# Moving the subtraction between the MLP's two products from VectorE to GpSimd

## What is computed

```
hid = jnp.square(jax.nn.relu(hn @ w_up))     # 1024 -> 4096
x   = x + hid @ w_down                        # 4096 -> 1024
```

## Time and profile before

| what | value |
|---|---|
| median of three executions | 1307.18 us (1299.17 to 1309.70) |
| profiled execution, span from first to last instruction | 1308.3 us |
| PE busy | 1250.8 us, 96% of the span |
| DVE busy | 679.0 us, 52% |
| POOL busy | 482.7 us, 37% |
| ACT busy | 430.3 us, 33% |

### The profile page before, as it was taken

One profiled execution on the slowest core, in us unless ns is written; L12 is line 12 of the kernel. 1 busy time (PEld: TensorE's weight loads), 2 busy tenths in 40 slices (PEclk: granted clock), 3 DMA queues, 4 the chain that ended last, 5 costly groups with the idle time before them and its releaser, 6 DMA issues.

```text
span 1308.3 us, 17577 instructions
## 1 busy us (share of the span) xinstructions
PE 1250.8 (96%) x6316; PEld 1036.0 (79%) x6316; DVE 679.0 (52%) x975; ACT 430.3 (33%) x764; POOL 482.7 (37%) x286
## 2 busy tenths in 40 slices
PE   5899999999898999999988999999999999999997
PEld 4787777688676888888878888888798888888886
DVE  5544366525997775875355711785672131321315
ACT  5444233235311423322334110442443232241331
POOL 3444111044233445344444323420235435344340
PEclk9999699999988999999988999999999999999999
DMA  6423000033553565565322311302223223323211
GB/s 210 130 81 111 3 2 1 1 99 128 161 163 111 199 212 169 182 219 177 113 97 92 111 65 65 90 1 81 65 101 125 82 92 103 110 74 118 80 51 64
DMA packets 71065, 135.32 MB, mean 103 GB/s; under 512 B 6947, under 2 KB 9763, under 8 KB 70987
## 3 DMA queue, kind: packets, MB, share of 16 engines
q1 hardware_dynamic: 53636, 98.10, 22.9%
q10 hardware_dynamic: 17358, 36.27, 8.4%
HBM read 131.44 MB, written 2.13 MB: 102 GB/s over the span
## 4 chain that ended last, share of the span: by engine, by line
PE 74%; DVE 13%; issue 6%; ACT 3%; POOL 2%; DMA 1%; ACTq 0%; DVEq 0%; POOLq 0%
PE gemm L874 21%; PE gemm L876 21%; PE gemm L875 21%; DVE mod_acc L1505 4%; POOL w_lo L442 2%; PE aux L1049 2%; PE aux L1233 2%; PE gemm L1012 1%; PE gemm L1004 1%; PE aux L1039 1%; PE aux L922 1%; PE gemm L1014 1%; DVE nmax L1620 1%; PE gemm L1193 1%; DVE prob_t L1387 1%
## 5 line engine op out<-in xcount | busy, mean ns | idle before, releaser
L442 POOL TENSOR_TENSOR w_lo<-w_raw,w_hi 128x1024 fp32r<-128x1024 f32 (+1 forms) x180 | 448.6, 2513 | 643.1 <-ACT w_hi L656 404.6
L874 PE MATMUL gemm<-xt_hi,w_hi 128*128 128x512 f32 (+1 forms) x704 | 256.8, 365 | 7.0 <-issue 4.9
L875 PE MATMUL gemm<-xt_lo,w_hi 128*128 128x512 f32 (+1 forms) x704 | 255.3, 363 | 0.0
L876 PE MATMUL gemm<-xt_hi,w_lo 128*128 128x512 f32 (+1 forms) x704 | 255.3, 363 | 0.0
L874 PE MATMUL gemm<-w_hi,ht_hi 128*128 128x512 f32 x512 | 203.2, 397 | 6.0 <-POOL w_lo L442 6.0
L875 PE MATMUL gemm<-w_lo,ht_hi 128*128 128x512 f32 x512 | 202.1, 395 | 0.0
L876 PE MATMUL gemm<-w_hi,ht_lo 128*128 128x512 f32 x512 | 202.0, 395 | 0.0
L656 ACT ACTIVATE w_hi<-w_raw 128x1024 fp32r<-128x1024 f32 x124 | 125.5, 1050 | 206.3 <-PE gemm L876 120.6
L874 PEld LDWEIGHTS gemm<-xt_hi,w_hi 128*128 128x128 f32 x704 | 134.7, 191 | 28.7 <-issue 6.1
L875 PEld LDWEIGHTS gemm<-xt_lo,w_hi 128*128 128x128 f32 x704 | 134.7, 191 | 20.1
L876 PEld LDWEIGHTS gemm<-xt_hi,w_lo 128*128 128x128 f32 x704 | 134.5, 191 | 20.2
(11 more groups left out here) (192 smaller groups left out, 1477.4 us busy)
## 6 DMA issues: line engine op xcount, KB each, us to landing
wm<-in_w_mod ACTq DMA_DIRECT2D x48, 512.0 KB, 4.5
w_raw<-in_w_in SPq DMA_DIRECT2D x32, 512.0 KB, 3.7
w_raw<-in_w_up SPq DMA_DIRECT2D x32, 512.0 KB, 3.6
w_raw<-in_w_down SPq DMA_DIRECT2D x32, 512.0 KB, 3.6
w_raw<-in_w_mlp_in SPq DMA_DIRECT2D x32, 512.0 KB, 3.7
w_raw<-in_w_mlp_out SPq DMA_DIRECT2D x32, 512.0 KB, 3.5
w_raw<-in_w_out SPq DMA_DIRECT2D x16, 512.0 KB, 3.5
x<-in_x SPq DMA_DIRECT2D x4, 512.0 KB, 7.7
```

Of the source, the lines that this page charges most:

```text
L442: pool.tensor_tensor(w_lo[s % 2][:, ks, 0:width], raw[q][:, :, 0:width], w_hi[s % 2][:, ks, 0:width].bitcast(F32), ALU.subtract).then_inc( ...
L874: pe.matmul(bank, lh, rh, start=(k == 0), stop=False)
L875: pe.matmul(bank, lh, rl, start=False, stop=False)
L876: mm = pe.matmul(bank, ll, rh, start=False, stop=(k == KT - 1))
```

## The change

The work between the two products is divided anew. ACT's second operation writes the unrounded square into `hid`. DVE makes `ht_hi` by one copy, which rounds. POOL makes `ht_lo` by the subtraction that DVE did. The relu's wait for `hid_hi` goes; the square waits until `ht_lo` of two tiles before is done, as `hid` has two buffers; ACT's wait at the end of the up tiles is for `hid_lo`. POOL's loop is written anew: `low(c)` of each chunk in the order before, with `hid_low(c - 1)`, the subtraction for tile c - 1, behind `low(c)` for c = 1 to 7, and `hid_low(7)` ahead of `low(8)`.

```diff
+            def hid_low(c, i, up0):
+                pool.wait_ge(hid_hi, i * 8 + (up0 + c + 1))
+                pool.tensor_tensor(ht_lo[:, c, :], hid[c % 2][:], ht_hi[:, c, :].bitcast(F32),
+                                   ALU.subtract).then_inc(hid_lo, 1)
+            def mlp(s0, up0, more):
+                def chunk(i, splits):
+                    for c in range(splits):
+                        s, q = s0 + c // 4 + 1, c % 4
+                        if c == 8:
+                            hid_low(7, i, up0)
+                        low(s, q, NC, i * 16 + (4 * s + q + 1))
+                        if 1 <= c < 8:
+                            hid_low(c - 1, i, up0)
+                with pool.Fori(0, NCH if more else NCH - 1) as i:
+                    chunk(i, 16)
+                if not more:
+                    chunk(NCH - 1, 12)
...
-            lows(SLAB_OUT1 + 1, SLAB_OUT2 - SLAB_OUT1)
+            lows(SLAB_OUT1 + 1, 2)
+            mlp(SLAB_MLP1, 0, True)
+            lows(SLAB_IN2 + 1, 4)
...
-            lows(SLAB_MLP2, SLABS - SLAB_MLP2)
+            lows(SLAB_MLP2, 1)
+            mlp(SLAB_MLP2, 8 * NCH, False)
...
                     if c >= 2:
                         act.wait_ge(hid_ready, i * 8 + (up0 + c - 1))
-                        act.wait_ge(hid_hi, i * 8 + (up0 + c - 1))
                     act.activation(relu[c % 2][:], gp[(t0 + c) % 4][:], ACT.Relu).then_inc(relu_done, 1)
                     act.wait_ge(relu_done, i * 8 + (up0 + c + 1))
-                    act.activation(ht_hi[:, c, :], relu[c % 2][:], ACT.Square).then_inc(hid_hi, 1)
+                    if c >= 2:
+                        act.wait_ge(hid_lo, i * 8 + (up0 + c - 1))
+                    act.activation(hid[c % 2][:], relu[c % 2][:], ACT.Square).then_inc(hid_ready, 1)
...
                     act.wait_ge(hid_ready, i * 8 + (up0 + 8))
-                    act.wait_ge(hid_hi, i * 8 + (up0 + 8))
+                    act.wait_ge(hid_lo, i * 8 + (up0 + 8))
...
-                            dve.wait_ge(relu_done, i * 8 + (up0 + c + 1))
-                            if c >= 2:
-                                dve.wait_ge(hid_lo, i * 8 + (up0 + c - 1))
-                            dve.tensor_tensor(hid[c % 2][:], relu[c % 2][:], relu[c % 2][:], ALU.mult
-                                              ).then_inc(hid_ready, 1)
-                            dve.wait_ge(hid_hi, i * 8 + (up0 + c + 1))
                             dve.wait_ge(hid_ready, i * 8 + (up0 + c + 1))
-                            dve.tensor_tensor(ht_lo[:, c, :], hid[c % 2][:], ht_hi[:, c, :].bitcast(F32),
-                                              ALU.subtract).then_inc(hid_lo, 1)
+                            dve.tensor_copy(ht_hi[:, c, :], hid[c % 2][:]).then_inc(hid_hi, 1)
```

More of the change, by code:

```diff
@@ L445, in lows @@
             def lows(first, slabs):
[L447 to L451, removed]
-                    for q in range(UQ):
-                        low(first + slabs - 1, q, NC, 4 * (first + slabs - 1) + q + 1)
+                for s in range(first, first + slabs):
+                    for q in range(UQ):
+                        low(s, q, NC, 4 * s + q + 1)
+            def hid_low(c, i, up0):
[15 more added lines that the diff above has]
+                    chunk(NCH - 1, 12)
             def clear_pads(q_pad, count):
@@ L1452, in chunk @@
                         if c < 8:
-                            dve.wait_ge(relu_done, i * 8 + (up0 + c + 1))
-                            if c >= 2:
-                                dve.wait_ge(hid_lo, i * 8 + (up0 + c - 1))
-                            dve.tensor_tensor(hid[c % 2][:], relu[c % 2][:], relu[c % 2][:], ALU.mult
-                                              ).then_inc(hid_ready, 1)
-                            dve.wait_ge(hid_hi, i * 8 + (up0 + c + 1))
                             dve.wait_ge(hid_ready, i * 8 + (up0 + c + 1))
-                            dve.tensor_tensor(ht_lo[:, c, :], hid[c % 2][:], ht_hi[:, c, :].bitcast(F32),
-                                              ALU.subtract).then_inc(hid_lo, 1)
+                            dve.tensor_copy(ht_hi[:, c, :], hid[c % 2][:]).then_inc(hid_hi, 1)
                         else:
                             dve.wait_ge(gemm_done, i * 16 + (t0 + c + 1))
-                            if c == 8:
-                                dve.wait_ge(hid_lo, i * 8 + (up0 + 8))
                             cols = acc[:, c % 4, (c // 4 - 2) * NC:(c // 4 - 1) * NC]
```

## The result

| | before | after |
|---|---|---|
| median of the runs | 1303.18 us (16 runs, 1296.41 to 1313.06) | 1315.53 us (16 runs, 1311.55 to 1326.60) |
| ratio | 1 | **1.0105** [1.0074, 1.0137] |
| DVE busy in the profiled execution | 679.0 us | 602.8 us |
| POOL busy | 482.7 us | 572.3 us |
| PE busy | 1250.8 us | 1240.7 us |

The change costs 12.35 us by the medians, where 12.6 us was forecast. One thing must be known to read the times: the executions of every kernel here fall into two groups 11 to 12 us apart. In the seven profiled executions whose time is of the lower group the first relu of the first MLP starts between 309.5 and 312.7 us, in the five of the upper group between 321.9 and 324.7, and those five have a stretch of 24 to 34 us at half clock from 140 us on. I call them **early** and **late**; the executions without a trace are sorted by their time alone.

The account below looks back on a forecast made before the run. PE was taken as the bound, except in the first MLP's chunk 0, where DVE's modulations set the pace. 6.8 + 2.8 + 1.7 + 1.3 = 12.6 us on 1307.2 gave 1319.8 us, range 1306 to 1327.

Parts of the forecast that it names:

- Tile 8 in seven chunks: PE's tile 8 waits 0.91 to 0.99 us for tile 6's subtraction behind low(7); together 6.8 us.
- Tile 4 in the second MLP: Chunk 0 there: two subtractions ahead of low(3) hold PE 2.8 us, and half clock after the pause costs 1.7 us.
- Chunk 0 of the first MLP: DVE's gain and loss cancel; tile 8 waits one more subtraction, +1.3 us, bounds -9.1 and +4.
- It is hidden by DVE's own lag: First MLP's chunk 0: tile 4 is held about 3 us, but DVE reaches it over 4 us behind relu.
- The two cancel to 0.7 us: First MLP's chunk 0: DVE saves 7.4 us and loses 8.1 us; DVE's short idle times cover the rest.
- The holding: First MLP's chunk 0: eight POOL subtractions each slow DVE's two-input accumulations by 1.0 us, 8.1 us in all.
- DVE's relief: First MLP's chunk 0: one copy replaces two DVE operations in each of eight tiles, saving 7.4 us.
- The skill's rule: First MLP's chunk 0: DVE fully blocked by each subtraction, 10.2 us lost, total 1321.9; the forecast used eight tenths instead.
- DVE's relief in chunk 0: Rival, first MLP: DVE keeps its 7.4 us, PE's waits shrink, a half-speed stretch goes; 1309.4 us, chance 0.20.
- The waits breed more: Rival: tile 4's delay shows in first-MLP chunks 0 and 1, or clock falls; 1325, dearest form 1332; chance 0.18.
- Never reaches PE: Rival: the new order does not delay PE, as when tile 7 ends later than read; 1307 us, chance 0.07.
- ACT's longer wait at the end of the up tiles: Some 1.7 us longer, hidden because tile 12 needs the splits behind it only 21.8 us later.

Follow-up runs that it names:

- e2: Changed kernel with ACT making splits 5, 6 and 7 one tile earlier, so low(7) ends before tile 6 needs POOL; ratio 1.0102 to the kernel before.
- e3: Changed kernel with both edits of order: subtractions for tiles 0 to 2 behind low(3), and splits 5 to 7 one tile earlier; ratio 0.9998 to the kernel before.
- e7: Changed kernel with POOL's subtraction for tile 6 ahead of low(7) instead of behind it; ratio 1.0071 to the kernel before.
- e6: Changed kernel with each of POOL's subtractions made twice in a row, the second one signalling; ratio 1.0376 to the kernel before.
- e1: Changed kernel with POOL's subtractions for tiles 0 to 2 moved behind low(3); ratio 1.0104 to the kernel before.
- e5: Changed kernel with each POOL subtraction covering 8 of 512 columns, the third pass reading ht_hi for ht_lo, order and waits kept; ratio 0.9952 to the kernel before.
- e10: e9 with ACT's splits 5 to 7 one tile earlier; ratio 0.9963 to the kernel before.
- e8: Kernel before the change with only ACT's splits 5 to 7 made one tile earlier; ratio 0.9968 to the kernel before.
- e4: Changed kernel with the subtraction back on DVE, DVE's copy kept and POOL left with its lows; ratio 0.9987 to the kernel before.
- e9: Changed kernel with ACT squaring twice, unrounded and rounded, DVE only subtracting and POOL left with its lows; ratio 0.9984 to the kernel before.

## Why the prediction was right, point by point

- **Tile 8 in seven chunks, 6.8 us: right.** The working gave 0.98 us in the second MLP; the chunks grew by 0.86, 0.86 and 0.95. In chunks 1 and 2 of the first MLP it was 1.21 and 1.25 instead of 0.91, since the subtraction there took 1.72 us (at 458.32) beside DVE's accumulations. e2 and e3 take it away in the second MLP, e7 takes a third off it there and e6 enlarges it.
- **Tile 4 in the second MLP, 4.5 us: right, 3.97 measured** (first relu to the eighth, 29.88 to 33.85 us). The wait was 2.36 us instead of 2.8. The first copy was held as forecast (1.05 us long, from 961.17) and its subtraction started 0.36 us after `low(1)`, 0.5 in the working; the second copy delayed `low(2)` by 0.2 us (2.59 long) instead of 0.5. The half clock was one stretch of 3.4 us, the 1.7 us taken. e1 removes all of it.
- **Chunk 0 of the first MLP, +1.3 us: the step that failed.** It was +3.95. "It is hidden by DVE's own lag" is wrong: tile 4 came out of a wait of 3.63 us (323.43), DVE began on that tile 23.7 us after the first relu (at 335.06) where it had been 20.9 (342.89), and the eight up tiles took 38.58 us instead of 35.87; the rest of the chunk, with tile 8, took 73.30 instead of 72.06. "The two cancel to 0.7 us" is wrong as well, by one of its two sizes. The holding was about right, 0.94 us each and 7.5 in all against 8.1. DVE's relief, forecast at 7.4 us, is worth 2.3 at most: nearly without the holding (e5) the chunk is only that much shorter than before, and PE waits at tile 8 for a split that still stands behind DVE's accumulations. So the subtractions cost the chunk 6.2 us (111.88 against 105.65) where at most 2.3 were gained. In e10 8 x 0.68 = 5.4 us less on DVE go with a chunk 5.3 us shorter, but by the table under e5 only 1.4 us of that are pauses and the rest is clock; what the relief is worth by itself is open.
- **The skill's rule.** By the Trainium skill (SBUF — State Buffer, "Who interferes with whom") the one that comes second is fully blocked. From this the prediction made 10.2 us of lost DVE time in chunk 0, as if DVE always came second. The measured loss is 7.5 us on DVE and 2.8 us on POOL's own eight (1.64 against 1.29 each): the trace agrees that either can hold the other, and 10.2 us on DVE alone was too much. Whether each overlap is lost in full no run here shows.
- **Between the MLPs, -1.9 us: not forecast.** The stage holds tile 8 of chunk 3, so about -2.8 is left. Before, PE ran at half clock for 6.8 us at 659.5 and 6.8 at 700.4 and 3.4 at 946.2; after, for 3.4 at 656.8 alone, while its waits there, without tile 8's, grew from 10.9 to 13.3 us. 13.6 us less at half clock are worth 6.8 us, against 2.4 of waits: the sign fits, and 1.6 us is left over. The other traces fit too: with 17.1 us at half clock the stage takes 357.77 to 358.40 us (before, e2, e7, e8), with 13.7 us 356.17 to 356.65 (e4, e5, e9, e10), with 6.8 us 356.10 and 356.62 (e1, e3). e7, in which this stage's work is that of the changed kernel, has 358.40, so the -1.9 us can't be put down to the change.
- **The sum.** 12.6 forecast and 12.0 in the traces is in part luck: chunk 0 was 2.6 too low, and the unforeseen -2.8 of one execution stood against it. The 12.35 of the medians is luck too, by the shares of early and late executions. The cost by groups, 15.6 and 14.9 us, is what the steps deserve: 12.6 and the 2.6 missed in chunk 0. Of the 3 us between that and the traces 2.0 are the favourable execution of after; About 1 us stays open. The forecast's level was off by more: 1307.18 was a median of three of which two were late, and the profiled execution of before was not 1.1 us over it but a late one of about 1310.1 (every listed execution's span is 1.8 us under its time).
- **The rivals.** DVE's relief in chunk 0 is at most 2.3 us, a quarter of the 9.1 it needed. "The waits breed more" was right at one place, tile 4 of chunk 0, and wrong on its dearest form: no half-speed stretch follows any of the waits of about 1 us in the second MLP. "Never reaches PE" is nearly what e3 made of the change by two edits of order.
- ACT's longer wait at the end of the up tiles was hidden as forecast: split 8 starts at 1260.60, and no wait of PE for its result is listed.

## What to carry to other kernels

A shared queue prices an added instruction by its place: the same 64 subtractions cost 12 to 15 us where the next matmul waits behind them and about 2 where it doesn't (e3 against e4), so find for each added instruction the consumer that is due right after it, and the slack it has in ns. When the input of a critical instruction can be made one tile earlier at no cost, do that before moving work between engines. When the times fall into groups, compare group with group: a median over both told of 12 us where it was 15, and left the 3 to 5 us that e10 gains in doubt. Taking work off an engine can pay only in the stretch where that engine sets the pace, and there an idle third engine (here ACT, 0.63 us for a second square) may take it more cheaply than one that holds it up (here POOL).

## What the runs showed of the hardware

- A copy from 32-bit floats to the rounded kind, 128x512 in SBUF, takes DVE 0.43 us (418 ns where nothing held it); the two-input subtraction of that shape takes 0.69. That is less than the 0.48 us of the one-input operation I priced it by.
- DVE and POOL slow each other both ways: in a loaded stretch 0.94 us of DVE for each POOL subtraction (after against e5), which take 1.64 us there and 1.29 elsewhere, and single copies up to 2.68 us.
- In the second MLP a wait of 2.36 us was followed by 3.4 us at 1.2 GHz (after), and none of the waits of about 1 us was. But of e6's four waits of 2.3 to 2.4 us at tile 8 only one was, so the length of a wait doesn't settle it. Between the MLPs the stretches at half clock differed from one trace to another, 17.1 us of them before and 3.4 after.
